# Two transformer stacks in one kernel on one core: the RMS norm's mean square taken per token, its root and reciprocal on a few columns, and the result spread by a product of ones with a diagonal

## What is computed

```python
def rmsnorm(t, g):
    tf = t.astype(jnp.float32)
    y = tf * lax.rsqrt(jnp.mean(tf * tf, axis=-1, keepdims=True) + EPS) * g.astype(jnp.float32)
    return y.astype(t.dtype)
```

## Time and profile before

| | |
|---|---|
| median of three runs | 2927.7 us |
| the profiled execution | 2928.85 us, span 2927.1 us |
| TensorE matmuls | 2716.9 us busy (93% of the span) |
| VectorE | 1806.9 us (62%) |
| ScalarE | 1452.9 us (50%) |
| mean granted TensorE clock | 0.953 |

### The profile page before, as it was taken

One profiled execution on the slowest core, in us unless ns is written; L12 is line 12 of the kernel. 1 busy time (PEld: TensorE's weight loads), 2 busy tenths in 40 slices (PEclk: granted clock), 3 DMA queues, 4 the chain that ended last, 5 costly groups with the idle time before them and its releaser, 6 DMA issues.

```text
span 2927.1 us, 38724 instructions
## 1 busy us (share of the span) xinstructions
PE 2716.9 (93%) x15354; PEld 2259.6 (77%) x15354; DVE 1806.9 (62%) x1895; ACT 1452.9 (50%) x1614; POOL 29.5 (1%) x40
## 2 busy tenths in 40 slices
PE   6999889999797999889779998799999999999998
PEld 3875358888695899777669986688888888888886
DVE  3224445553535576573345555498888888888886
ACT  3226224332335354532134444377777777777775
POOL 0001000000002000000000000000000000000000
PEclk8999999999898999996889999899999999999999
DMA  7446312222231344420024451299999999999996
GB/s 288 186 182 262 132 71 89 113 100 80 78 127 50 147 173 159 153 87 1 1 86 173 168 191 61 101 361 344 360 347 360 340 339 366 341 362 347 347 361 227
DMA packets 84359, 590.07 MB, mean 202 GB/s; under 512 B 9872, under 2 KB 10000, under 8 KB 19472
## 3 DMA queue, kind: packets, MB, share of 16 engines
q1 hardware_dynamic: 82800, 576.43, 53.1%
q10 hardware_dynamic: 1440, 11.93, 1.0%
HBM read 587.27 MB, written 1.05 MB: 201 GB/s over the span
## 4 chain that ended last, share of the span: by engine, by line
PE 84%; DVE 9%; ACT 4%; issue 2%; DMA 1%; ACTq 0%; POOL 0%; DVEq 0%; SPq 0%; POOLq 0%
PE banks L461 22%; PE banks L462 21%; PE banks L463 21%; PE banks L467 17%; DVE ring_rounded L523 2%; DMA ring<-in_stream 1%; ACT ring_rounded L513 1%; PE banks L2637 1%; DVE rstd L738 1%; PE banks L826 1%; DVE activations L1322 1%; DVE aT L751 0%; ACT scratch L903 0%; DVE aT L2061 0%; DVE nmax L869 0%
## 5 line engine op out<-in xcount | busy, mean ns | idle before, releaser
L523 DVE TENSOR_TENSOR ring_rounded<-ring,ring_rounded 128x2048 fp32r<-128x2048 f32 (+3 forms) x164 | 330.3, 2017 | 453.6 <-ACT ring_rounded L513 452.7
L462 PE MATMUL banks<-ring_rounded,activations_rounded 128*128 128x512 f32 x1344 | 527.9, 393 | 0.0
L462 PE MATMUL banks<-aT_rounded,ring_rounded 128*128 128x256 f32 (+1 forms) x1568 | 507.1, 323 | 0.0
L513 ACT ACTIVATE ring_rounded<-ring 128x2048 fp32r<-128x2048 f32 (+3 forms) x164 | 276.7, 1691 | 394.9 <-PE banks L463 386.6
L461 PE MATMUL banks<-aT_rounded,ring_rounded 128*128 128x256 f32 (+2 forms) x1120 | 338.8, 303 | 22.7 <-DVE aT_rounded L760 11.6
L463 PE MATMUL banks<-aT_rounded,ring_rounded 128*128 128x256 f32 (+2 forms) x1120 | 336.3, 300 | 0.0
L462 PEld LDWEIGHTS banks<-aT_rounded,ring_rounded 128*128 128x128 f32 x1568 | 305.6, 195 | 21.1
L462 PEld LDWEIGHTS banks<-ring_rounded,activations_rounded 128*128 128x128 f32 x1344 | 252.8, 188 | 52.2
L2811 DVE TENSOR_TENSOR ring_rounded<-ring,tables_rounded 128x2048 fp32r<-128x2048 f32 x112 | 253.5, 2288 | 23.5 <-ACT tables_rounded L2729 23.3
L2729 ACT ACTIVATE tables_rounded<-ring 128x2048 fp32r<-128x2048 f32 x112 | 214.9, 1920 | 94.6 <-DMA ring<-in_stream 84.5
L2811 DVE TENSOR_TENSOR ring_rounded<-ring,aT_rounded 128x2048 fp32r<-128x2048 f32 x112 | 253.9, 2286 | 11.8 <-ACT aT_rounded L2729 11.5
(11 more groups left out here) (316 smaller groups left out, 4867.9 us busy)
## 6 DMA issues: line engine op xcount, KB each, us to landing
ring<-in_stream SPq DMA_DIRECT2D x501, 1024.0 KB, 5.3
ring<-in_stream SPq DMA_DIRECT2D x32, 704.0 KB, 5.6
ring<-in_stream SPq DMA_DIRECT2D x28, 768.0 KB, 6.1
activations<-in_rpb ACTq DMA_DIRECT2D x2, 1536.0 KB, 6.3
ring<-in_stream SPq DMA_DIRECT2D x6, 512.0 KB, 5.0
tables<-in_tab_b ACTq DMA_DIRECT2D x1, 2436.0 KB, 8.7
tables<-in_tab_a ACTq DMA_DIRECT2D x1, 2304.0 KB, 8.6
hT<-in_h ACTq DMA_DIRECT2D x1, 2048.0 KB, 15.7
```

The source lines that it names most:

```text
L462: pe.matmul(out, exact(upper), exact(w_lower), start=False, stop=False)
L513: act.activation(exact(upper), w, ACT.Copy).then_inc(g.s["act_pieces"], 1)
L523: dve.tensor_tensor(exact(w), w, rounded(upper), ALU.subtract).then_inc(g.s["dve_pieces"], 1)
```

## The change

It leaves ("n1", 0) as it is and changes the other nine norms:

- `sum_pe` swaps the operands. The squares of 128 tokens are the weights, two columns of the `mean` table are what moves. A tile takes T/128 such products (4 or 2), each with its own weight load of 128x128, and each leaves 2 equal columns in PSUM with tokens on the partitions.
- The root and the reciprocal work on 2T/128 columns (8 or 4) in a new small buffer `rtok`.
- VectorE multiplies the identity, repeated T/128 times, by the reciprocals, each repeated over 128 columns. That writes T/128 diagonal matrices side by side into `rstd`.
- A new function `spread_pe` waits for them, multiplies a table of ones as weights with those T columns, and so has the reciprocal root of each token in all 128 rows of a second PSUM bank of the kind `long`.
- L751 reads the reciprocal roots from that bank rather than from `rstd` in SBUF.

```diff
@@ squares_act
-    act.activation(g.rstd[:, 0:T], g.bank(("mean square", key))[:, 0:T], ACT.Sqrt, bias=g.eps[:, 0:1]).then_inc(g.s["act_norm"], 1)
+    to, n = (g.rstd, T) if key == ("n1", 0) else (g.rtok, T // 64)
+    act.activation(to[:, 0:n], g.bank(("mean square", key))[:, 0:n], ACT.Sqrt, bias=g.eps[:, 0:1]).then_inc(g.s["act_norm"], 1)
@@ sum_pe
-    mm(pe, ps[:, 0:T], g.tab("mean"), g.sq[:, k % SQUARES, 0:T], k == first, k == KD - 1).then_inc(g.s["pe_norm"], 1)
+    if key == ("n1", 0):
+        mm(pe, ps[:, 0:T], g.tab("mean"), g.sq[:, k % SQUARES, 0:T], k == first, k == KD - 1).then_inc(g.s["pe_norm"], 1)
+        g.count("pe_norm", ("summed", key, k))
+        return
+
+    for c in range(T // P):
+        last = mm(pe, ps[:, 2 * c:2 * c + 2], g.sq[:, k % SQUARES, P * c:P * c + P], g.tab("mean")[:, 0:2],
+                  (k, c) == (first, 0), (k, c) == (KD - 1, T // P - 1))
+    last.then_inc(g.s["pe_norm"], 1)
     g.count("pe_norm", ("summed", key, k))
+    if k == KD - 1:
+        spread_pe(g, pe, key, T)
+
+
+def spread_pe(g, pe, key, T):
+
+    pe.wait_ge(*g.bank_free("long"))
+    ps = g.open(("rstd", key), "long")
+    pe.wait_ge(g.s["dve_norm"], g.at("diagonal", key))
+    mm(pe, ps[:, 0:T], g.tab("ones"), g.rstd[:, 0:T]).then_inc(g.s["pe_norm"], 1)
+    g.count("pe_norm", ("mm", "rstd", key))
@@ rstd_dve
-    dve.reciprocal(g.rstd[:, 0:T], g.rstd[:, 0:T]).then_inc(g.s["dve_norm"], 1)
+    if key == ("n1", 0):
+        dve.reciprocal(g.rstd[:, 0:T], g.rstd[:, 0:T]).then_inc(g.s["dve_norm"], 1)
+        g.count("dve_norm")
+        return
+
+    n = T // P
+    dve.reciprocal(g.rtok[:, 0:2 * n], g.rtok[:, 0:2 * n]).then_inc(g.s["dve_norm"], 1)
     g.count("dve_norm")
+    dve.wait_ge(g.s["dve_norm"], g.so_far("dve_norm"))
+    ident = g.tab("ident").unsqueeze(1).broadcast_to((P, n, P))
+    r = g.rtok[:, 0:2 * n].rearrange("p (c two) -> p c two", two=2)[:, :, 0:1].broadcast_to((P, n, P))
+    dve.tensor_tensor(g.rstd[:, 0:T].rearrange("p (c t) -> p c t", c=n), ident, r, ALU.mult).then_inc(g.s["dve_norm"], 1)
+    g.count("dve_norm", ("diagonal", key))
@@ norm_dve
-    dve.wait_ge(g.s["dve_norm"], g.so_far("dve_norm"))
+        dve.wait_ge(g.s["pe_norm"], g.at("mm", "rstd", key))
+        rstd = g.bank(("rstd", key))
+    else:
+        dve.wait_ge(g.s["dve_norm"], g.so_far("dve_norm"))
+        rstd = g.rstd
...
-            dve.scalar_tensor_tensor(dst[:, k, c], src[:, k, c], scales(k, s), g.rstd[:, c],
+            dve.scalar_tensor_tensor(dst[:, k, c], rstd[:, c], scales(k, s), src[:, k, c],
...
+        g.also("dve_norm", ("free", ("rstd", key)))
```

More of the change, by code:

```diff
@@ L3164, in build @@
         g.cend = g.sb("chunk_ends", 4, 8)
-        g.rstd, g.eps = g.sb("rstd", T2), g.sb("eps", 4)
+        g.rstd, g.eps, g.rtok = g.sb("rstd", T2), g.sb("eps", 4), g.sb("token_rstd", 2 * T2 // P)
         g.nmax, g.rsum, g.rinv = g.sb("nmax", 2, 2), g.sb("rsum", 2, 2), g.sb("rinv", 2, 2)
```

## The result

The changed kernel takes 2940.09 us (median of 7 runs, 2936.42 to 2943.74) against 2926.6 for the kernel before on the same chip. The ratio is 1.0048, 95% interval 1.0036 to 1.006. The prediction, 2926.2 with no measurable change as the likeliest outcome, is wrong: the change is slower by 13.5 us, outside the range. The profiled execution took 2941.37 us, span 2939.6, mean granted clock 0.951 (0.953 before).

The account below looks back on a forecast made before the run. TensorE was taken to bound the kernel, with VectorE counting only where TensorE waits, as at norms. Terms -2.0 - 1.25 - 0.84 + 2.1 + 0.5 gave -1.5 us: 2927.35 for the execution, 2926.2 as median, range 2920.5 to 2930.

Parts of the forecast that it names:

- The sum: Over the whole kernel: terms for the changed norms, -2.0 - 1.25 - 0.84 + 2.1 + 0.5 = -1.5 us.
- costed at nothing: Effects taken as free: tile 6's narrow products, the wait for the second `long` bank, TensorE's wait for the diagonals.
- The norms of 256 tokens: At ("n2", 1), "ffn0", "mix1", "ffn1": 0.56 us less at full clock, taken as 0.5 each, 2.0 less together.
- "mix0" and "last": Norms with eight squares on TensorE: low clock for 32 narrow products, 2.1 us more at "mix0", 0.5 at "last".
- ("n2", 0) and ("n1", 1): Norms of 512 tokens between products: 1.25 us less at ("n2", 0), 0.84 less at ("n1", 1).
- the middle taken: At ("n2", 0): 1.25 us less, between 1.69 at full clock and 0.84 with the spread after the clock's fall.
- My 1.0 us for the clock: Projection behind "mix0": starts at half clock instead of running its first 1.1 us at full, 1.0 us more.
- The first (narrow products raise the clock): At "mix0" and "last", narrow products raise and hold the clock as wide ones do: 2922.2 us; chance 0.13.
- The second (the clock isn't lost in the gap): Ahead of projections, the spread product divides the gap and the clock stays: 8.1 us saved, 2918.1 us; chance 0.10.
- The third: In the norms, the diagonal multiplication runs at the reciprocal's rate: 13.2 us more, 2939.4 us; chance 0.05.
- the prediction's signs of being wrong: PEclk rising during "mix0"'s 32 records, projections after ("n2", 1), "ffn0" or "mix1" starting at 1.00, long roots or diagonals.

Follow-up runs that it names:

- e1: Kernel before plus one unused 32-byte tile behind eps, so activations and scratch begin 32 bytes further: 2943.57 us, before 2927.58.
- e2: The whole change, with its new tile allocated last, behind scratch, instead of in the middle of SBUF: 2920.47 us, ratio to before 0.9975.
- e8: e4 with vectors allocated behind tables instead of ahead, so tables begins at 114816 instead of 117312: 2909.69 us, ratio to before 0.9947.
- e4: e2 with the old norm (wide products) at "mix0" and "last": 2919.41 us, ratio to before 0.9979.
- e5: Kernel before with chunk_ends allocated last, so activations and scratch begin 128 bytes earlier: 2939.92 us, before 2925.69.
- e7: Kernel before with 32 unused bytes between activations and scratch, shifting scratch alone: 2932.68 us, ratio 1.0028.
- e9: Kernel before with only vectors allocated behind tables, so tables begins at 114816 instead of 117312: 2917.35 us, before 2925.25.
- e3: Changed kernel with its new tile 16 floats wide instead of 8, so activations and scratch begin 64 bytes further than before: 2935.22 us, ratio 1.0026.

## Why the prediction was wrong

**The step that failed** is the one that wasn't there. The sum goes from the norms to the total as if every product that the change doesn't touch kept its duration, and the list of what is "costed at nothing" lacks the allocation of `rtok`. In the runs it is the largest term: 2943.57 - 2927.58 = 16 us by itself (e1), and within the change 2940.1 less e2's 2920.5, some 20 us by medians that weren't taken side by side, or 17.3 by the sums of the table below. Everything else is smaller.

**The norms of 256 tokens.** Right in mechanism and size for the chain from the last square to the first scaling: 0.56 us forecast at full clock and 0.15 with the spread product at 1.2 GHz, 0.60 read at ("n2", 1), "ffn0" and "ffn1" and 0.44 at "mix1". In e2, where the clock falls before the spread product of "mix1", only 0.07 is left there. But a term is missing behind them. In "ffn0" the low-clock stretch that the projection runs into is shorter. These are stretches of the kernel before, and then of the changed one, which comes there some 5 us later:

```profile
1513.70:1520.40 6.70, 5.95 (x28) 5.98 (x29) 5.33 (x15) 3.05 (x8) 0.00 (x0) 0.50 0.29 124
1520.60:1524.00 3.40, 3.40 (x31) 3.40 (x30) 0.00 (x0) 0.82 (x1) 0.00 (x0) 1.00 0.02 5
```

```profile
1518.90:1522.10 3.20, 3.01 (x14) 3.04 (x15) 3.20 (x10) 1.67 (x4) 0.00 (x0) 0.50 0.61 259
1522.30:1525.50 3.20, 3.20 (x29) 3.20 (x28) 1.44 (x4) 0.82 (x2) 0.00 (x0) 1.00 0.00 0
```

The clock is low for 3.4 us (1518.75 to 1522.16) instead of 6.8 (1513.63 to 1520.46). The prediction asked only whether the clock would be kept or lost, and gave the loss its whole old length. All six profiles of the changed norms show this at "ffn0" and none of the seven of the old norms does. At ("n2", 1) four of the six show it, and two of the seven. The table has the times in us between the starts of the first scalings of the norms, so each row holds the second norm's own chain. It starts at ("n2", 0) because profiles lie up to 9 us apart when they get there (388.2 us in e8, 397.2 in e2):

| from, to | before | changed | e2 | e4 |
|---|---|---|---|---|
| ("n2", 0), ("n1", 1) | 382.62 | 388.11 | 381.13 | 380.85 |
| ("n1", 1), ("n2", 1) | 205.40 | 204.84 | 204.93 | 204.68 |
| ("n2", 1), ("final", 1) | 206.30 | 204.84 | 204.49 | 204.47 |
| ("final", 1), "mix0" | 10.08 | 11.83 | 11.82 | 11.41 |
| "mix0", "ffn0" | 312.57 | 312.25 | 312.70 | 313.00 |
| "ffn0", "mix1" | 199.06 | 196.24 | 197.73 | 197.77 |
| "mix1", "ffn1" | 162.33 | 161.69 | 161.04 | 161.08 |
| "ffn1", "last" | 1042.06 | 1053.62 | 1042.29 | 1039.48 |

From ("n2", 0) to "last" e2 is 4.3 us below before, and with the 1.7 us of ("n2", 0)'s own chain 6.0, where the medians say 7.1. The forecast was -0.2 and, with ("n2", 0), -1.5. So with the tile in the right place it was too high as well, by some 4.5 us. Of these 1.2 lie behind ("n2", 1) (1.8 less the own chain of ("final", 1)), 0.8 each between "ffn0" and "mix1" and between "mix1" and "ffn1" (the row's saving less the 0.5 that the sum had for it), 0.6 behind ("n2", 0) and 0.4 in its own chain. "mix0" and "last" make the rest. The prediction took the stretches behind these norms as unchanged.

How much of that the new norms do is open, since the timing of an execution moves these rows too. From ("n2", 1) to ("final", 1) three kernels with the old norms take 204.64 (e1), 205.14 (e5) and 205.19 us (e7), where before takes 206.30 and the six with the new norms 204.47 to 204.86. From "ffn0" to "mix1" the two kinds stay apart: 197.95 to 199.06 with the old norms, 196.24 to 197.78 with the new ones. The changed column shows the two dense stages with the extra: 7.0 and 11.3 us more than e2.

**("n2", 0) and ("n1", 1).** Right: -1.67 and -0.86 us where -1.25 and -0.84 were forecast, the first at the full-clock value (-1.69) rather than at the middle taken.

**"mix0" and "last".** Right about the clock: it stays at 0.50 through the narrow records and on into the projection. The narrow products cost 0.59 us more than the wide ones in "last" (forecast 0.60), though with other timings the wide ones do better or worse, as e4's chain of 7.82 and e9's of 8.97 us show, so the close match has luck in it. "mix0" took 1.75 us more to its first scaling in the changed kernel, from which the 0.60 goes off that ("final", 1) came earlier, and it lost 0.28 behind (-0.32, of which -0.60 is the own chain of "ffn0"): 1.4 instead of 2.1. In e2 it is 1.9. But it is no loss that wide products would take back. With the new norms ahead, wide products in "mix0" come to 11.41 + 313.00 in e4 and 11.47 + 313.05 in e8, against 11.82 + 312.70 in e2 with narrow ones. Stretches of e2 and then of e4, from the products through the projection:

```profile
1190.40:1197.20 6.80, 6.80 (x32) 6.76 (x32) 5.00 (x4) 2.43 (x8) 0.00 (x0) 0.50 0.08 35
1201.20:1206.30 5.10, 5.10 (x24) 5.10 (x25) 4.60 (x14) 2.51 (x6) 0.00 (x0) 0.50 0.00 0
```

```profile
1184.80:1191.40 6.60, 5.74 (x14) 4.62 (x15) 5.96 (x6) 3.40 (x10) 0.00 (x0) 0.50 0.23 96
1191.60:1194.80 3.20, 0.62 (x3) 0.19 (x2) 2.00 (x2) 0.47 (x1) 0.00 (x0) 1.00 0.00 0
1196.10:1201.60 5.50, 5.50 (x26) 5.50 (x27) 4.69 (x14) 2.51 (x6) 0.00 (x0) 0.50 0.00 0
```

The wide products do raise the clock, but for a stretch in which TensorE has 0.62 us of work. Then it falls again, and the projection runs at half speed for 5.5 us as in e2. In the kernel before the rise came in time for the first 1.1 us of the projection. My 1.0 us for the clock was a price of timing, and not of the products: e1, e5 and e7, with the old norms and wide products, miss the rise as well, and from ("final", 1) to "ffn0" they take 324.2 to 324.6 us, as long as e2's 324.5, where before takes 322.65.

**The rivals.** None of the three happened. The first (narrow products raise the clock) is refuted by the two rows of 0.50 above; that e2's 2920.5 is near its 2921.5 is chance. The second (the clock isn't lost in the gap) didn't happen at any site; what did happen is a shorter low stretch. The third is out by the 424 ns of L769. What made the kernel slower, placement, was in none of them. Nor did any of the prediction's signs of being wrong appear: PEclk stays at 0.50 through the 32 records, the projections start at 0.50, and roots and diagonals are short. All of them watch the norms, and the loss was elsewhere.

**What stays open.** The rule (the same place within 256 bytes) is shown by the kernel's times for `ring` against `activations` and `scratch` together, by e7 for `scratch`, and by e8 and e9 for `tables` against `activations`. Which read delays which isn't shown. That the next product's weight load and the running product's moving columns get in each other's way is an argument from the steps in e5, wasn't tried by itself, and two runs speak against it as the whole story. In e1 the steps from a product of `aT` (in its place) to one of `activations` (off) took 230.8 ns, where those in e5 took 226.1. In e3 even the steps from one product of `aT` to the next, with the weights of both in `ring`, took 232.4 ns (143), where those in e1 and e5 took 225.8 and 225.9. Steps between products of 256 columns didn't slow down (median 120 ns before and after, means 120.0 and 119.3). Behind the norms, two things changed together: the gap ahead of the projection is shorter, and the spread product now stands in it. No run has one without the other, so which of them shortens the low-clock stretch isn't shown, and at ("n2", 1) e5 and e7 have the short stretch with neither.

## What to carry to other kernels

A change has a part that no diff of the instructions shows: where its new buffer pushes the others. Allocate new small tensors last, or take care that the tensors which TensorE reads in turn keep their distance to each other modulo 256 bytes. Here 32 bytes lost 16 us, and `tables` put in step gained 8 to 10 us over kernels in which no view of busy time had shown a fault. Where TensorE is 100% busy at full clock before and after, count the products in a fixed stretch: 884 against 866 says what TensorE's busy share can't. When the gap ahead of a projection changes, ask how long the low clock behind it will last, not only whether it comes. And before a difference of 1 or 2 us in one stage is put down to a change, see how far that stage varies between kernels that are alike there.

## What the hardware did that I had not expected

- 32 bytes of shift between the tensors cost 4.7 ns a product, on average, in the feed-forward of 512-column products (steps of 226.7 and 231.4 ns) and 0.6% of the whole kernel (e1, ratio 1.0058). In that stretch 64 bytes cost 6.3 ns (200.4/860 = 233.0) and 128 bytes 2.6 ns (200.4/874 = 229.3); 256 bytes cost nothing (884 products, as before).
- Moving everything together by 32 bytes costs nothing (ratio 1.0).
- Behind "ffn0" the low-clock stretch lasted 3.4 us in all six profiles of the changed norms and 6.8 us in all seven of the old ones. The time from the end of the last square's product to the projection was 3.36 us there instead of 3.87, with the spread product in it.
